# Second block's input products in plain fp32 inside the first block's stretch, and the LRU's gates from 64-row products, in a two-branch encoder layer on Trainium2

## What is computed

```
z = rmsnorm(x) @ w_in                       # 1024 -> 1536: xl, gl, us of 512 each
xc = causal_conv4(xl)
r, ig = sigmoid(xc @ wa), sigmoid(xc @ wx)  # 8 heads, one 64x64 matrix for each head and gate
a = exp(-8 r softplus(-lambda))
h[t] = a[t] h[t-1] + sqrt(1 - a[t]^2) ig[t] xc[t]
y_lru = h * gelu(gl)
ys = S5(us)                                 # 32 groups, 16 inputs, 64 complex states each
g = gelu(ys);  y_ssm = g * sigmoid(g @ w_glu)
x += [rmsnorm(y_lru), rmsnorm(y_ssm)] @ w_out
x += (silu(h2 @ w_gate) * (h2 @ w_up)) @ w_down    # h2 = rmsnorm(x), 1024 -> 2816 -> 1024
y = rmsnorm(x)
```

## Time and profile before

| what | value |
|---|---|
| median of three executions | 2329.43 us (2329.09 to 2330.92) |
| the profiled execution, its own time | 2331.18 us |
| its span | 2329.4 us |
| PE busy | 2205.3 us (95%) |
| DVE busy | 1542.1 us (66%) |
| ACT busy | 1090.7 us (47%) |
| POOL busy | 410.2 us (18%) |
| first gate product of block 0 at full flow | 283.06 us |

### The profile page before, as it was taken

One profiled execution on the slowest core, in us unless ns is written; L12 is line 12 of the kernel. 1 busy time (PEld: TensorE's weight loads), 2 busy tenths in 40 slices (PEclk: granted clock), 3 DMA queues, 4 the chain that ended last, 5 costly groups with the idle time before them and its releaser, 6 DMA issues.

```text
span 2329.4 us, 30360 instructions
## 1 busy us (share of the span) xinstructions
PE 2205.3 (95%) x11650; PEld 2119.3 (91%) x11650; DVE 1542.1 (66%) x2581; ACT 1090.7 (47%) x1458; POOL 410.2 (18%) x459
## 2 busy tenths in 40 slices
PE   4876799999999999999999999999999999999996
PEld 2555799999999999999999999999999999999996
DVE  8667546578756656875766578766658875665544
ACT  3444434654634455564444664644455563432232
POOL 6433101024011101321010023111102321100001
PEclk9977899999999999999999999999999999999998
DMA  5762333546333545553353655334455643343331
GB/s 171 210 169 77 115 117 115 152 154 191 123 111 117 176 125 162 168 166 109 117 172 106 151 175 174 127 113 141 152 138 156 173 135 109 117 147 109 124 121 58
DMA packets 200527, 322.81 MB, mean 139 GB/s; under 512 B 89088, under 2 KB 131712, under 8 KB 200256
## 3 DMA queue, kind: packets, MB, share of 16 engines
q1 hardware_dynamic: 200256, 320.65, 45.5%
q0 software_dynamic: 128, 0.23, 0.0%
HBM read 296.39 MB, written 26.53 MB: 139 GB/s over the span
## 4 chain that ended last, share of the span: by engine, by line
PE 88%; DVE 5%; POOL 2%; ACT 2%; issue 1%; DMA 1%; SPq 1%; POOLq 0%; DVEq 0%; ACTq 0%
PE acc L814 27%; PE acc L816 27%; PE acc L815 26%; PE acc L879 3%; PE acc L901 1%; POOL tmp L545 1%; PE acc L900 1%; PE acc L910 1%; DVE rstd L1093 1%; PE acc L890 1%; PE acc L872 1%; DVE w_hl L976 1%; DVE s5prod L976 0%; DMA u<-z_dram 0%; DVE act_hl L976 0%
## 5 line engine op out<-in xcount | busy, mean ns | idle before, releaser
L814 PE MATMUL acc<-act_hl,w_hl 128*128 128x416 f32 x2544 | 905.1, 356 | 18.1 <-DVE act_hl L976 18.1
L816 PE MATMUL acc<-act_hl,w_hl 128*128 128x416 f32 x2544 | 895.2, 352 | 0.0
L815 PE MATMUL acc<-act_hl,w_hl 128*128 128x416 f32 x2544 | 892.4, 351 | 0.0
L976 DVE TENSOR_TENSOR w_hl<-w_raw,w_hl 128x1024 fp32r<-128x1024 f32 x428 | 532.0, 1257 | 78.9 <-ACT w_hl L634 77.6
L814 PEld LDWEIGHTS acc<-act_hl,w_hl 128*128 128x128 f32 x2544 | 479.9, 189 | 29.1 <-issue 16.3
L815 PEld LDWEIGHTS acc<-act_hl,w_hl 128*128 128x128 f32 x2544 | 480.0, 189 | 9.7 <-issue 5.0
L634 ACT ACTIVATE w_hl<-w_raw 128x1024 fp32r<-128x1024 f32 x428 | 443.6, 1051 | 78.6 <-DMA w_raw<-in_w_in 43.4
L816 PEld LDWEIGHTS acc<-act_hl,w_hl 128*128 128x128 f32 x2544 | 479.7, 189 | 0.6
L976 DVE TENSOR_TENSOR x_acc<-x_acc,acc 128x416 f32<-128x416 f32 x480 | 272.9, 585 | 199.1 <-PE acc L816 192.3
L545 POOL TENSOR_TENSOR tmp<-tmp 128x416 f32<-128x416 f32 x135 | 168.3, 1246 | 1123.3 <-ACT tmp L642 1113.3
L814 PE MATMUL acc<-ff_hl,w_hl 128*128 128x416 f32 x880 | 312.3, 355 | 14.8 <-DVE x_acc L976 12.0
(11 more groups left out here) (155 smaller groups left out, 1894.2 us busy)
## 6 DMA issues: line engine op xcount, KB each, us to landing
w_raw<-in_w_ffn SPq DMA_DIRECT2D x330, 512.0 KB, 3.7
w_raw<-in_w_in SPq DMA_DIRECT2D x60, 512.0 KB, 3.4
w_raw<-in_w_out SPq DMA_DIRECT2D x40, 512.0 KB, 3.3
s5y<-y_dram SPq DMA_DIRECT2D x80, 256.0 KB, 4.1
s5t<-t_dram SPq DMA_DIRECT2D x64, 162.0 KB, 3.9
s5v<-v_dram SPq DMA_DIRECT2D x80, 128.0 KB, 3.8
x_acc<-in_x SPq DMA_DIRECT2D x4, 1664.0 KB, 7.3
out_y<-x_acc SPq DMA_DIRECT2D x8, 832.0 KB, 6.5
```

The costliest lines, as they stand in the source:

```text
L814: pe.matmul(out, w(0), x(0), start=first, stop=False)
L815: pe.matmul(out, w(0), x(1), start=False, stop=False)
L816: return pe.matmul(out, w(1), x(0), start=False, stop=last)
L976: return v.tensor_tensor(out, x, y, op)
```

## The change

The twelve input products of block 1 leave the feed-forward part of block 0 and stand in `FIRST`, in plain fp32 (`raw`), with the load of its x, its norm and its normalised rows. Their results wait in new buffers (`zs_next`, `kept`) laid over ones that are idle then; a step `xc` copies the kept xl rows back. `SECOND` is the table that weaves the rest of block 1's mixer. `MIXER`, for blocks 2 to 4, stays. The norm of the input of blocks 0 and 1 is summed by eight fp32 matmuls with ones instead of POOL's additions. In all norms ACT now takes the root out of PSUM and DVE the reciprocal after it. `ga` uses 64-row products: one head's 64 rows against both gates' matrices. `FIRST` is otherwise reordered too (`pq` and `pb` ahead of most squares, `glu` ahead of `oa`, three `oa` behind `ns`).

```diff
@@ the order
+SECOND = [(26, ('xc', 0)), (26, ('cv', 0)), (27, ('xc', 1)), (27, ('cv', 1)), (27, ('ga', 0)), (27, ('bx', 0)), (27, ('zl', 0)), (28, ('ga', 1)), (29, ('bx', 1)), ...
-FIRST = [('x', 0), ('pa', 0), ('sq1', 0), ('sq1', 1), ('sq1', 2), ('sq1', 3), ('tb', 0), ('pq', 0), ('pb', 0), ('n1', 0), ...
+FIRST = [('x', 0), ('pa', 0), ('sq1', 0), ('pq', 0), ('pb', 0), ('sq1', 1), ('sq1', 2), ('tb', 0), ('sq1', 3), ('n1', 0), ...
...
-                out += [(kind, b + 1, j) for at, (kind, j) in MIXER if at == place]
+                out += [(kind, b + 1, j) for at, (kind, j) in (MIXER if b else SECOND) if at == place]
@@ which units are raw
+def raw(kind, b, j):
+    return kind in ("us", "xl", "gl") and b < 2
@@ SP
                 if kind == "x" and b:
                     if b >= 2:
                         sp.wait_ge(y_st[b % 2], 32 * (b // 2))
+                    else:
+                        sp.wait_ge(pl_done, 1)
@@ ACT
-            def root(which, b):
-                act.wait_ge(rec_done, NORM_N[(which, b)] + 1)
-                act.activation(rstd[:], rstd[:], ACT.Sqrt).then_inc(rstd_done, 1)
+            def root(step):
+                bank, tk = wait_m(act, step), width(step[1])
+                act.activation(root_of(step, tk), acc[:, bank, 0:tk], ACT.Sqrt, bias=sm(EPSC), scale=1.0 / (NCH[step[0]] * P))\
+                   .then_inc(m_freed(step), 1)
...
+                elif kind == "xc":
+                    act.wait_ge(conv_done, b * KL + j)
+                    act.activation(xl[:, 3:3 + tk], kept[:, KL + j, 0:tk], ACT.Copy).then_inc(xc_done, 1)
...
-                    for g, (slot, bias) in enumerate(((6, B_A), (0, B_X))):
-                        bank = wait_m(act, (*step, g))
-                        act.activation(tmp[:, slot + j % 2, :], acc[:, bank, 0:T], ACT.Sigmoid, bias=v1(bias + j))\
-                           .then_inc(m_freed((*step, g)), 1)
+                    for h in range(2):
+                        own, other = (slice(0, NP_), slice(NP_, P)) if h == 0 else (slice(NP_, P), slice(0, NP_))
+                        bank = wait_m(act, (*step, h))
+                        act.activation(tmp[own, 6 + j % 2, 0:tk], acc[own, bank, 0:tk], ACT.Sigmoid, bias=vec[own, B_A + j:B_A + j + 1])
+                        act.activation(tmp[own, j % 2, 0:tk], acc[other, bank, 0:tk], ACT.Sigmoid, bias=b_swap[other, j:j + 1])\
+                           .then_inc(m_freed((*step, h)), 1)
@@ PE
+                    if not sums(kind, b):
+                        bank = m_bank(step)
+                        for k in range(KD):
+                            pe.wait_ge(sq_done, SQ_AT[(kind, b)] + k + 1)
+                            ins = pe.matmul(acc[:, bank, 0:tk], ones[:], first_sq(b, k), start=k == 0, stop=k == KD - 1)
+                        ins.then_inc(m_full, 1)
+                        continue
...
-                    if b == 0:
+                    if b < 2:
                         for k in range(KD):
                             if j == 0:
-                                pe.wait_ge(h_made, k + 1)
-                            ins = pe.matmul(acc[:, bank, 0:T], w_raw[UNIT[step] % RING][:, k * P:(k + 1) * P],
-                                            rows[:, k, :], start=k == 0, stop=k == KD - 1)
+                                pe.wait_ge(h_made, h_at("h1", b) + k + 1)
+                            ins = pe.matmul(acc[:, bank, 0:tk], w_raw[UNIT[step] % RING][:, k * P:(k + 1) * P],
+                                            rows(b)[:, k, 0:tk], start=k == 0, stop=k == KD - 1)
...
-                    for g in range(2):
-                        bank = m_bank((*step, g))
-                        pe.matmul(acc[:, bank, 0:T], w_gates[:, g, j, :], tmp[:, 4 + j % 2, :], start=True, stop=True)\
+                    banks = [m_bank((*step, h)) for h in range(2)]
+                    for h in range(2):
+                        r = slice(h * NP_, (h + 1) * NP_)
+                        pe.matmul(acc[:, banks[h], 0:tk], w_gates[r, j, :], tmp[r, 4 + j % 2, 0:tk], start=True, stop=True)\
                           .then_inc(m_full, 1)
@@ DVE
-            def reciprocal_mean(step):
-                bank = wait_m(v, step)
-                v.tensor_scalar(rstd[:], acc[:, bank, 0:T], 1.0 / (NCH[step[0]] * P), EPS, MUL, ADD).then_inc(m_freed(step), 1)
+            def reciprocal_root(step):
                 wait_evacuated(v, step)
-                v.reciprocal(rstd[:], rstd[:]).then_inc(rec_done, 1)
+                tk = width(step[1])
+                v.reciprocal(root_of(step, tk), root_of(step, tk)).then_inc(rstd_done, 1)
```

More of the change, by code:

```diff
@@ L49, with width, cols5, here @@
 RING, LEAD_HI, LEAD_LO = 6, 3, 2
-assert TPL + TS == T and TPL % L == 0
+assert TPL + TS == T and TPL % L == 0 and T0 % L == 0 and T0 <= T
+C50 = T0 // L
+def width(b):
+    return T if b else T0
+def cols5(b):
+    return width(b) // L
+def here(b):
+    return slice(T0 + (b - 1) * T, T0 + b * T) if b else slice(0, T0)
 IN_ORDER = [("us", 0), ("us", 1), ("us", 2), ("us", 3), ("xl", 0), ("xl", 1), ("gl", 0), ("gl", 1),
@@ L65, in steps @@
 def steps():
-    out = [(kind, 0, j) for kind, j in FIRST] + [("x", 1, 0)]
+    out = [(kind, b[0] if b else 0, j) for kind, j, *b in FIRST]
     for b in range(NB):
@@ L98, with split_here @@
 NU = len(SRC)
[L100 to L105, removed]
+EARLY = 4
+def raw(kind, b, j):
+    return kind in ("us", "xl", "gl") and b < 2
+SPLIT = {u: i for i, u in enumerate(u for u, s in enumerate(SRC) if not raw(*s))}
+OWN = list(SPLIT)[:2 + EARLY]
+assert [SRC[u] for u in OWN] == [("glu", 0, 0), ("glu", 0, 1)] + [("out", 0, j) for j in range(EARLY)]
+def split_here(u):
+    return u < NU and u in SPLIT and u not in OWN
 def early(kind, b, j):
@@ L137, with sums @@
 NCH = {"n1": KD, "nl": KL, "ns": KL, "n2": KD, "nf": KD}
+def sums(which, b):
+    return 0 if which == "n1" and b < 2 else NCH[which] - 1
 SQ_AT = {n: sum(NCH[w] for w, _ in NORMS[:i]) for i, n in enumerate(NORMS)}
-SUM_AT = {n: sum(NCH[w] - 1 for w, _ in NORMS[:i]) for i, n in enumerate(NORMS)}
+SUM_AT = {n: sum(sums(*w) for w in NORMS[:i]) for i, n in enumerate(NORMS)}
 NORM_N = {n: i for i, n in enumerate(NORMS)}
+H_AT = {n: i * KD for i, n in enumerate((k, b) for k, b, j in STEPS if k in ("h1", "h2") and j == 0)}
+HL_AT = {n: i * KD for i, n in enumerate(n for n in H_AT if not (n[0] == "h1" and n[1] < 2))}
 def build(nc, a, outs):
@@ L552, in _ @@
                     for m in (2 * j, 2 * j + 1):
-                        if m:
+                        if m and sums(which, b):
                             sum_up(which, b, m)
@@ L637, in square @@
                 n = SUM_AT[(which, b)]
+                if not sums(which, b):
+                    act.activation(first_sq(b, k), src, ACT.Square).then_inc(sq_done, 1)
+                    return
                 if k >= 2:
@@ L1155, in _ @@
                 kind, b, j = step
[L1156 removed]
+                tk = width(b // NPAIR if kind == "dn" else b)
+                if step in PLACE and split_here(PLACE[step] + LEAD_LO):
                     weight_lo(PLACE[step] + LEAD_LO)
                 elif kind == "wc":
[L1159 removed]
+                    weight_lo(OWN[j])
                 if kind in ("gate", "up", "dn"):
```

296 lines of the change are left out of this document (167 added, 129 removed).

## The result

The changed kernel takes **2347.5 us** (median of 7 runs, 2340.1 to 2353.4) where the kernel before took 2329.1 (7 runs, 2326.7 to 2330.9): a ratio of 1.0079, 95% interval 1.0063 to 1.0094. It is slower by 0.8%, where 1.2% faster was forecast.

A forecast was written before the change was run, and what follows sets the result against it. PE was taken to bound the full stream, chains of waits the stretch from 98 to 283 us. From the profiled 2331.2 us, -54 + 3 + 28 - 3 - 1 gave 2304.2, against the median 2302.5 us; range 2284 to 2326.

The forecast's parts named there:

- term 1: Block 0's feed-forward part: twelve units leave it, -54 us, with +3 us for doubled waits of PE for DVE.
- Term 2, the later begin: First stretch, with block 1's products moved in: block 0's first gate comes at 311 instead of 283 us, +28 us.
- (a): Start of the first stretch: first product at 30.2 instead of 33.5 us.
- (b): S5 inputs in the first stretch: first S5 matmul at about 114 instead of 123.4 us, PE idle some 10 us before.
- (d): From `nl` to the first `gate`: 71 us instead of 81.3, so the first gate at 311 us.
- (c): From first S5 matmul to `nl`: 115 us of PE work plus waits, so `nl` at 240 instead of 201.8 us.
- Term 3: Gate pairs of the other four blocks: 64-row products save 0.2 us each over 16 pairs, -3 us.
- Term 4: End of the kernel: last norm loses its mean on DVE, -1 us; norms of blocks 2 to 4 covered by products.
- Tight fill: Rival: first-stretch gaps take nearly all twelve products, first gate at 295 us; 2287 us, chance 0.13.
- Gate pairs side by side: Rival: both 64-row products of a gate pair run in parallel, gates' term at -11 us; 2294 us, chance 0.15.
- Products at half clock: Rival: moved products in the first stretch run at half clock, slower than before; 2337 us, chance 0.11.
- DVE binds: Rival: in the thinned S5 part of block 1's mixer PE waits for DVE, 15 us given back; 2318 us, chance 0.18.

The follow-up runs named there:

- e11: Changed kernel with 128-row gates and two sigmoids, root first only in block 0 and at `n1` of block 1, `s5in` ahead of the ring of weights: 2315.7 us.
- e12: As e11, but with the change's 64-row gate products and four 64-partition sigmoids: 2326.0 us.
- e9: Changed kernel with `s5in` laid ahead of the ring of weights, restoring the old distance between weights and moving operand: 2337.3 us.
- e3: Changed kernel with the old order at every norm, mean and reciprocal on VectorE, ScalarE's root behind: 2350.2 us.
- e10: Kernel before with only `s5in` laid behind `rstd`, as the change does it: 2340.8 us.
- e13: Separate kernel, TensorE alone repeating a unit's three products on zeros for 75 address and distance pairs: 13.63 to 13.73 us per 72 products.
- e6: Kernel before with the 32 bytes of `lru_st` placed behind the ring of weights instead of ahead of it: 2347.4 us.
- e14: As e11, but each of a gate pair's two sigmoids cut into two of 64 partitions, products still 128 rows: 2325.6 us.

## Why the prediction was wrong

Four steps lead from the kernel before to the changed one; between the profiled runs, from the start to the last `nf`, they are: before to e11 is -14.5 us (the move, with root first in the first stretch), e11 to e12 +8.9 (gates), e12 to e9 +11.2 (root first behind the first stretch), e9 to after +11.3 (layout). Together +16.9, and in timed medians -14.2, +10.3, +11.3, +10.2. I had -27 for the whole. What failed is that two costs were put at nothing (ACT's sigmoids, and ACT's root on the way of blocks 1 to 4), that a third had no term (the layout), and that the gain of term 1 was too large.

- **Term 2, the later begin, was right, and the gates spoilt it.** With 128-row gates (e11) `n2` of block 0 comes 27.4 us later than before and the first gate 26.9 (309.9 us); I had +28. In the changed kernel `n2` comes 36.2 us later: `nl` at 248.1 instead of my 240, the first gate at 318.6 instead of 311. (a) and (b) hold: first product 28.6 (30.2), first S5 matmul 112.1 (114) after 9.6 us of waiting (10). (d), 71 us from `nl` to the first gate, holds too (70.5). What failed is (c), "three gate pairs at 1.4": the pairs cost PE little, but behind them it waits for ACT and loses clock.
- **Term 1, the shorter part, was 8 us too large.** -42.6 instead of -51; with the layout, the gates and the norms restored it is -44.5 (e11). From the first gate to `n2` of block 1 e11 takes 347.1 us and the kernel before 391.1: 44 us less, where the twelve products alone are 54. Of the missing 10 us 6.5 are waits, twice what I had: PE is idle 9.7 us there instead of 3.2 (for `x_acc` 2.2 us once, for ACT's S5 output 2.2 us once). The rest is clock. In e11 it drops to its lower level twice for 3.4 us, once just after the wait for ACT's S5 output and once after a wait of 0.9 us, which costs half of 6.8 us:

```profile
450.00:500.00 50.00, 46.42 (x255) 43.69 (x254) 42.72 (x94) 28.52 (x40) 11.53 (x18) 0.97 0.45 137
500.00:550.00 50.00, 48.55 (x289) 47.53 (x287) 39.33 (x100) 24.28 (x35) 21.37 (x29) 0.97 0.63 203
```

  Before, the clock was full from 371 to 803 us.
- **Term 3, the gates, had the wrong sign: -3 forecast, +10 measured.** Its bounds went from -11 to +8, all on PE. On PE it was right in sign: in blocks 1 to 4 a pair takes 0.90 us from its start to the next unit's instead of 1.27 on average, 6 us for 16 pairs. The failing sentence is "24 us more ACT in the whole kernel, hidden where ACT is at 51%". A share over the span doesn't hide an instruction that stands in ACT's order between a PE product and the bank that the next PE product waits for.
- **Term 4 was the sentence "their norms are covered by products", cost nothing.** It cost 11.3 us (e9 against e12), in the pieces from `nl` to `ns` above all. PE doesn't wait for the norm's own result, that is true. But each engine works in its own order, and so hands the wait on. DVE's and PE's timelines of the changed kernel at `nl` of block 3:

```profile
1447.28 2.75 DVE L1197 RECIPROCAL rstd<-rstd 128x416 f32<-128x416 f32 x1 [3.02 <-ACT rstd L735]
1449.95 1.16 DVE L1080 TENSOR_TENSOR w_hl<-w_raw,w_hl 128x1024 fp32r<-128x1024 f32 x1
```

```profile
1451.71 0.43 PE L909 MATMUL acc<-ff_hl,w_hl 128*128 128x416 f32 x1 [1.53 <-DVE w_hl L1080]
```

and ACT's, ahead of it:

```profile
1443.23 0.52 ACT L902 ACTIVATE f_g<-acc 128x416 f32<-128x416 f32 x1 [1.18 <-PE acc L911]
1443.77 1.28 ACT L860 ACT_TABLE_LOAD   x1
1445.07 0.26 ACT L860 ACTIVATE u<-acc 128x104 f32<-128x104 f32 x1
1445.34 1.28 ACT L735 ACT_TABLE_LOAD   x1
1446.64 0.61 ACT L735 ACTIVATE rstd<-acc,small 128x416 f32<-128x416 f32 x1
```

  Before, the same place read, first DVE and then ACT:

```profile
1439.93 0.59 DVE L1091 TENSOR_SCALAR rstd<-acc 128x416 f32<-128x416 f32 x1 [0.56 <-PE acc L872]
1440.56 2.75 DVE L1093 RECIPROCAL rstd<-rstd 128x416 f32<-128x416 f32 x1
```

```profile
1455.06 0.55 ACT L646 ACTIVATE rstd<-rstd 128x416 f32<-128x416 f32 x1
```

  DVE waited 0.56 us for PE's product, and ACT's root came 15 us behind the mean, with nothing late for it. Now DVE waits 3.02 us for ACT, which first has a Silu and a Gelu to do with a table load each, then its own. DVE's split of a weight is queued behind the reciprocal, and PE waits for that.
- **The layout had no term.** I read the diff's new place of `s5in` as memory and not as time. It cost 10.2 us.
- **The rivals.** *Tight fill* had the first gate at 295 us; it came at 318.6. *Gate pairs side by side*: the pairs did get shorter, by 0.17 to 0.65 us, but ACT's sigmoids cost more than that. *Products at half clock*, my slower case, didn't happen: the clock was 0.87 from 98 to 202 us, and the first gate at 319, before its point of 337. The result has the sign of this rival by other causes. *DVE binds*: PE's waits for it from the first gate to `n2` of block 1 are 2.2 us at most and 8.0 in all, 5 more than before, not 15.
- **The signs I named**: "waits of PE for DVE above 10 us" didn't occur, "a first gate after 325" neither. The sign "the part of block 0 shorter by 51 to 54 us" failed (42.6), and so did the block periods "less 0.8": from `n2` of one block to that of the next they are 8.0, 5.6 and 8.5 us longer. That last sign is the one that pointed to the terms that failed.

## What to carry to other kernels

An engine at half load is no cover for an instruction that stands, in its order, between a product and the buffer that the next product waits for: count it at that place. Keep a slow in-order engine out of the path of a result that nobody waits for, and put it back on the path only where the other engine is the one waited for (here root first won 8 us in the first stretch, e3 against the changed kernel, and lost 11 behind it; e11 keeps both halves right and is faster than both kernels, 2315.7 us). And when an edit moves a buffer, time the old program with the new layout alone (e10) before explaining anything else: 10 of the 18 us lost were that.

## What the runs showed of the hardware that I had not expected

- The spacing of fp32r products (128 columns of weights, 416 moving) depends on the distance in bytes between weights and moving operand: 13.63 us for 72 at 32 modulo 128, 13.71 to 13.73 elsewhere, with only TensorE running (e13). In the kernels it was 187.4 to 189.8 ns, and 32 bytes changed the whole by 19 us (e6). The Trainium skill (TensorE: Matmul & The Clock Gate, Back-to-back issue gap) gives for the isolated gap of one product the columns over 2.4 GHz plus 2.5 ns, by which an estimate for 416 columns is 176 ns, says that in a stream the weight loads count too, and states no dependence on addresses. The full streams here have 187.4 ns at best. Their weight loads (PEld) take 187 to 189 ns each on the profile's page, near the spacing; which of the two sets it was not tested.
- A pair of 64-row products takes PE 0.90 us, a pair of 128 rows 1.07 to 1.55 (1.27 on average, blocks 1 to 4), and no gain in the whole time stands clear of the noise (2326.0 us in e12, 2325.6 in e14).
- A sigmoid of 64 partitions takes ACT as long as one of 128: 603 and 604 ns for 416 elements.
- Short waits can cost more by the clock than by themselves: from 150 to 202 us e12 idles 3.2 us more than e11, and is granted 0.87 of the clock instead of 1.00, 7 us of work less. It isn't always so: e14 idles 2.9 us more than e11 there, at 0.93.
